# More warm-up products on TensorE, and five operations put elsewhere, at the start of a hybrid decoder layer

## The reference, cut to what matters

```python
xn = rmsnorm(h, norm_mix)
z = xn @ w_in                      # (1072 tokens x 1024) @ (1024 x 3592)
y_a = z[B] * causal_conv(z[C] * z[H])
q, k, v = silu(causal_conv(z[QKV]))
g    = -exp(a_log) * softplus(z[O_A:O_A + 4] + dt_bias)   # 4 columns of w_in
beta = sigmoid(z[O_A + 4:O_A + 8])                        # 4 more
o = gated_delta_rule(l2norm(q), l2norm(k), v, g, beta, state)
h = h + concat(y_a, rmsnorm(o) * silu(z[G])) @ w_out
h = h + relu(rmsnorm(h, norm_ffn) @ w_up) ** 2 @ w_down
y = rmsnorm(h, norm_final)
```

## Time and profile before

| | us |
|---|---|
| median of 3 runs | 1337.58 |
| lowest and highest | 1337.32, 1339.33 |
| the profiled execution's own time | 1337.32 |
| its span, first to last instruction | 1335.5 |
| PE busy in that span | 1315.9 (99%) |
| mean granted clock of PE | 0.998 |

### The profile page before, as it was taken

The page is one execution under the profiler, slowest core; times in us unless marked ns, Lnnn a source line. Parts: engine busy times, 40 slices in busy tenths (PEclk is TensorE's granted clock), DMA queues, the critical chain, the costliest instruction groups (busy, mean ns, idle before and its releaser), DMA issues.

```text
span 1335.5 us, 22540 instructions
## 1 busy us (share of the span) xinstructions
PE 1315.9 (99%) x9035; PEld 1287.1 (96%) x9035; DVE 832.0 (62%) x1406; ACT 410.8 (31%) x805; POOL 523.9 (39%) x544
## 2 busy tenths in 40 slices
PE   7999999999999999999999999999999999999997
PEld 6899999899999999999999999999999999999997
DVE  5566798435453665556666656756667567666855
ACT  6566552111221213231122222322223222223312
POOL 2322112111111111221367465574574756746811
PEclk9999999999999999999999999999999999999999
DMA  6223562743323323221101212112121121111202
GB/s 193 58 77 90 155 174 65 206 117 87 88 64 82 101 57 89 81 65 48 49 32 49 64 33 64 33 54 58 33 64 48 48 64 33 48 48 48 75 38 114
DMA packets 161850, 99.88 MB, mean 75 GB/s; under 512 B 19639, under 2 KB 156371, under 8 KB 161746
## 3 DMA queue, kind: packets, MB, share of 16 engines
q1 hardware_dynamic: 138770, 85.56, 21.8%
q10 hardware_dynamic: 22976, 12.88, 3.6%
HBM read 77.62 MB, written 20.80 MB: 74 GB/s over the span
## 4 chain that ended last, share of the span: by engine, by line
PE 96%; DVE 2%; ACT 1%; issue 0%; DMA 0%; ACTq 0%; POOL 0%; DVEq 0%
PE banks L1343 10%; PE banks L1345 10%; PE banks L1344 10%; PE banks L1854 9%; PE banks L1856 9%; PE banks L1855 9%; PE banks L1873 7%; PE banks L1874 7%; PE banks L1872 7%; PE banks L1888 1%; PE banks L1889 1%; PE banks L1890 1%; PE banks L1550 1%; PE banks L1564 1%; PE banks L1784 1%; PE banks L1466 1%
## 5 line engine op out<-in xcount | busy, mean ns | idle before, releaser
L1854 PE MATMUL banks<-hg_high,w_high 128*128 128x384 f32 (+1 forms) x768 | 249.5, 325 | 0.0
L1856 PE MATMUL banks<-hg_high,w_low 128*128 128x384 f32 (+1 forms) x768 | 247.6, 322 | 0.0
L1855 PE MATMUL banks<-hg_low,w_high 128*128 128x384 f32 (+1 forms) x768 | 247.3, 322 | 0.0
L2550 DVE TENSOR_TENSOR hT<-hT,banks 128x528 f32<-128x528 f32 x280 | 189.4, 701 | 84.4 <-PE banks L1874 77.3
L1343 PE MATMUL banks<-xn_high,w_high 128*128 128x384 f32 (+1 forms) x672 | 226.8, 337 | 0.8 <-DVE xn_low L1955 0.7
L1345 PE MATMUL banks<-xn_high,w_low 128*128 128x384 f32 (+1 forms) x672 | 218.1, 325 | 0.0
L1344 PE MATMUL banks<-xn_low,w_high 128*128 128x384 f32 (+1 forms) x672 | 217.9, 324 | 0.0
L786 POOL TENSOR_TENSOR w_low<-w_raw,w_high 128x1024 fp32r<-128x1024 f32 x31 | 77.0, 2483 | 244.4 <-ACT w_high L980 244.4
L1854 PEld LDWEIGHTS banks<-hg_high,w_high 128*128 128x128 f32 x768 | 144.2, 188 | 1.9 <-POOL w_low L912 1.7
L1855 PEld LDWEIGHTS banks<-hg_low,w_high 128*128 128x128 f32 x768 | 144.3, 188 | 0.1
L1856 PEld LDWEIGHTS banks<-hg_high,w_low 128*128 128x128 f32 x768 | 144.2, 188 | 0.0
(11 more groups left out here) (321 smaller groups left out, 2780.5 us busy)
## 6 DMA issues: line engine op xcount, KB each, us to landing
w_raw<-in_w_up SPq DMA_DIRECT2D x32, 512.0 KB, 4.0
w_pair<-in_w_down SPq DMA_DIRECT2D x32, 512.0 KB, 3.4
w_raw<-in_w_in SPq DMA_DIRECT2D x28, 512.0 KB, 4.3
w_raw<-in_w_out SPq DMA_DIRECT2D x8, 512.0 KB, 3.9
x_slice<-in_x_prompt SPq DMA_DIRECT2D x8, 512.0 KB, 4.1
out<-y_tok SPq DMA_DIRECT2D x8, 512.0 KB, 2.6
x_tok<-in_x_prompt SPq DMA_DIRECT2D x2, 1536.0 KB, 10.0
v_kept_rows<-v_feat SPq DMA_DIRECT2D x4, 536.0 KB, 2.9
```

The costliest lines, as they stand in the source:

```text
L1854: pe.matmul(bank[:, 0:w], w_h[half][:, k, :], hg_h[:, k, c0:c0 + w], start=(k == 0), stop=False)
L1855: pe.matmul(bank[:, 0:w], w_h[half][:, k, :], hg_l[:, k, c0:c0 + w], start=False, stop=False)
L1856: ins = pe.matmul(bank[:, 0:w], w_l[half][:, k, :], hg_h[:, k, c0:c0 + w], start=False, stop=(k == KT - 1))
L2550: dve.tensor_tensor(hc, hc, both, ALU.add if sign > 0 else ALU.subtract).then_inc(acc_read_dve, 1)
```

## The change

Six edits:

1. `IDLE_PRODUCTS` goes from (3, 1, 1) to (6, 4, 2): 7 more products ahead of tiles 0, 1 and 2.
2. SP issues `ab_raw` behind the two large loads of the tiles 3 to 8, not ahead of them.
3. ACT makes the high part of `ab` behind the square of tile 4, not right behind `split_high(0)`.
4. POOL makes the low part of `ab` behind the powers of tiles 0 to 5, not behind tile 2's.
5. DVE makes the low part of the first weight block behind the first `xn_low`, not ahead of it.
6. SP's send of the `v` rows goes from `g == 1` to `g == 2`, behind the load of a weight block.

PE's program is otherwise unchanged: `made_ab(0)` stays ahead of `turn_x(8)`.

```diff
-        IDLE_PRODUCTS = (3, 1, 1)
+        IDLE_PRODUCTS = (6, 4, 2)
...
-                if g == 1 and n >= 9 and IN_TILES[n - 1][0] == "v":
+                if g == 2 and n >= 9 and IN_TILES[n - 1][0] == "v":
...
                 if n == 0:
-                    sp.dma_start(ab_raw[:, :, :], w_in_v[:, :, O_A:O_A + 8]).then_inc(s_ahead, 16)
                     sp.dma_start(x_big[:, 2:5, :], xp_v[:, 2:5, :]).then_inc(s_xin[3], 16)
                     sp.dma_start(x_big[:, 5:8, :], xp_v[:, 5:8, :]).then_inc(s_xin[4], 16)
+                    sp.dma_start(ab_raw[:, :, :], w_in_v[:, :, O_A:O_A + 8]).then_inc(s_ahead, 16)
...
-            for t in range(NT):
+            for t in GTILES[0] + GTILES[1]:
                 x_power(t)
-                if t == 2:
-                    pool.wait_ge(ab_hi, 1)
-                    pool.tensor_tensor(ab_w[:, :, 8:16], ab_raw[:, :, :], ab_w[:, :, 0:8].bitcast(F32),
-                                       ALU.subtract).then_inc(ab_lo, 1)
+            pool.wait_ge(ab_hi, 1)
+            pool.tensor_tensor(ab_w[:, :, 8:16], ab_raw[:, :, :], ab_w[:, :, 0:8].bitcast(F32),
+                               ALU.subtract).then_inc(ab_lo, 1)
+            for t in GTILES[2]:
+                x_power(t)
...
             split_high(0)
-            act.wait_ge(s_ahead, 16)
-            act.activation(ab_w[:, :, 0:8], ab_raw[:, :, :], ACT.Copy).then_inc(ab_hi, 1)
...
                 for t in SQUARE_AFTER.get(m, ()):
                     square_x(t)
+                    if t == 4:
+                        act.wait_ge(s_ahead, 16)
+                        act.activation(ab_w[:, :, 0:8], ab_raw[:, :, :], ACT.Copy).then_inc(ab_hi, 1)
...
-            dve.wait_ge(w_high, 1)
-            dve.tensor_tensor(w_l[0][:, :, :], w_raw[0][:, :, :], w_h[0][:, :, :].bitcast(F32),
-                              ALU.subtract).then_inc(w_low, 1)
...
+                if m == 0:
+                    dve.wait_ge(w_high, 1)
+                    dve.tensor_tensor(w_l[0][:, :, :], w_raw[0][:, :, :], w_h[0][:, :, :].bitcast(F32),
+                                      ALU.subtract).then_inc(w_low, 1)
```

## The result

| | before | after |
|---|---|---|
| median of 6 runs each, us | 1337.51 | 1349.37 |
| lowest and highest | 1337.15, 1339.85 | 1347.35, 1352.31 |
| ratio, 95% interval | | 1.0078 [1.0061, 1.0093] |
| the profiled execution's own time | 1337.32 | 1350.52 |
| its span | 1335.5 | 1348.7 |

The change costs 11.9 us by the medians and 13.2 us between the two profiled executions. The ratio is taken over all executions on record, 23 of the kernel after (1345.33 to 1353.36 us, median 1347.69), and makes it 10.4 us. Each of these is at least twice the 5.0 us of my sum, and the time is outside my range.

The account below looks back on a forecast made before the run. TensorE was taken as the bound, its dense matmuls from 28.3 us on, so a late start is late at the end. 2.3 + 2.7 = 5.0 us on 1337.32, with the median's 0.26: 1342.5 us, range 1340.1 to 1344.1.

Parts of the forecast that it names:

- my sum: Whole kernel: 2.3 us for the later start of tile 2 plus 2.7 for the `ab` step, 5.0 us slower.
- my range: Whole kernel's time: the forecast's own range, 1340.1 to 1344.1 us around 1342.5.
- Edit 6: SP's v send behind a weight block's load: no PE stall to shorten from 70 to 200 us, 0, up to 0.3 either way.
- the clock falls in the new stall: Rival, chance 0.15: PE's clock drops while waiting ahead of `made_ab(0)`, at least +2.3 us, so 1344.9.
- d: Delay of tile 2's first transpose from seven more products ahead of it: +2.3 us (0.8 to 3.1, far end 5.5).
- The `ab` step: Late split of `ab` holds `made_ab(0)` and the transposes behind it: ninth high part +2.7 us (1.7 to 3.4) beyond d.
- POOL's low part: POOL's low part of `ab`, behind tile 5's power: taken near its old row of 1.21 us, ending at 22.2 plus d.
- Edit 5: DVE's weight split behind the first low part: 1.2 us by itself, partly hidden as an input of the `ab` step.
- Edit 2: `ab_raw` loaded behind the big loads: covered by eight high parts and two squares, cost 0, 0 to +1 us.
- the same busy time by stretch from 70 us on: Expected sign in the new profile: busy times by stretch unchanged from 70 us on.

Follow-up runs that it names:

- experiment 6: The whole changed kernel with only the fourth v send put back ahead of the weight load: 1345.66 us against 1338.99 before, ratio 1.0043.
- experiment 2: The kernel before with the late load and split of `ab` alone (edits 2, 3 and 4): 1340.78 us against 1337.81, ratio 1.0022.
- experiment 1: The kernel before with edit 6 alone, the v sends moved to `g == 2`: 1345.67 us against 1337.81, ratio 1.0056.
- second kernel of experiment 10: The kernel before with `turn_ab` in three parts and no idle products, (0, 0, 0): 1338.35 us against 1337.78, ratio 1.0002.
- experiments 5 to 8: Edit 6 plus products in its stall; change with fourth send back; `ab` step with transposes first; before with fewer products: 1342.37, 1345.66, 1340.88, 1337.42 us (first run).

## Why the prediction was wrong, by its steps

- **Edit 6, "PE has no stall from 70 to 200 us that an earlier load could shorten: 0, and as far as it goes, up to 0.3 either way": the step that failed.** Alone it costs 0.56% (7.5 us by the ratio). I asked what the load gains from going first, not who waits for the send that goes second. DVE's wait for the fourth send is one line of code, and SP's waits for the solve that now stand ahead of it are in the same step. I also looked at a window that ended at 200 us, while the send is used at 234. With the fourth send alone put back, the ratio of 1.0043 makes about 1343.3 us, inside my range; but that is partly luck, since the start was later there than I had summed.
- **The rival "the clock falls in the new stall": right as an extra, not in place of the sum.** The fall came behind the stall ahead of `made_ab(0)`, as said, at a price of 3.9 - 2.2 = 1.7 us against my 2.3. I had not asked it of any other place, since I had foreseen one stall. The clock falls also behind the second one, where in the profile of after it costs more than the wait (4.16 against 2.88 us), and behind `turn_ab` (+1.54), which may be chance.
- **d, +2.3 (0.8 to 3.1, far end 5.5): mis-sized for the profiled execution, and not a fixed number.** 0.9 after, 0.4 to 0.6 alone at the bound, 3.5 in experiment 6, all with the same products. The reason for the low end was the one given: the rise comes earlier. The sensitivity to it was right.
- **The `ab` step, +2.7 (1.7 to 3.4): inside its range by luck, from two errors of opposite sign.** The ninth high part is 4.27 us late (26.37 against 22.10). Without d of 0.9 that is 3.4, my high end; without the clock's 1.7 as well, 1.7 us are left, my low end. POOL's low part was the term too large: 1.21 assumed, 0.31 to 0.48 measured. It also started earlier than I had worked out, at 21.53 in after, which is 20.6 without d, against 21.05 to 21.7. With DVE's weight split no longer beside it, the low part is short. The Trainium skill ("SBUF — State Buffer", the part on the shared port pair) says that of a GpSimd operation that reads SBUF and a DVE operation with two SBUF inputs or in a two-port mode, the one that starts second is blocked until the other has ended. The numbers agree with it: 1.21 us beside a DVE operation with two SBUF inputs, ending 0.18 us behind it; 0.31 in experiment 2, where it started 0.07 us ahead of DVE's scaling.
- **Edit 5, hidden in the `ab` step: right.** PE waits 1.6 us for `w_low` where it waited 0.38, and alone it moves the bound by 0.2.
- **Edit 2, 0 to +1: right, with little room.** In experiment 2 `ab_raw` landed 12.6 us after its issue and ACT took it at once; in after it landed at 18.1 us (13.7 after its issue at 4.41), and ACT came for it at 19.11.
- **My own signs of error.** I had named "PE's stall ahead of `made_ab(0)` under 2 us" (it is 2.4), "tile 2 before 13" (13.36), and an end not late by as much as the two (it is later). None of these could catch edit 6. The sign that did was the last of the list before them, "the same busy time by stretch from 70 us on": it held to 200 us and broke at 245.

## What to carry to other kernels

When a DMA is moved, find every wait on its semaphore, and read the queue between its old and its new place for waits on other engines; a late wait in the same step is worse than the load it made way for. In this kernel every new stall of PE of 2.4 to 4.0 us came with a stretch at the lower clock, which at the stalls for `v_meta` cost as much again as the wait or more. So each stall in a forecast needs that term, with work for PE as the cure if the wait can't go. Work that fills a wait has a value that its own rows don't show: ask what the engine will do in that time once the work is elsewhere.

## What the runs showed of the hardware

- The lower level came back with PE never idle: 63.47 to 66.88 us after a row of 18 products of 16x8 in 2.13 us. The stretches at the lower level lasted 3.4 us in most places, 6.7 in experiment 2, and 10.2 behind the stalls for `v_meta` in after and experiment 1. In after PE was busy for 2.85 us of the first 3.42 of these and all the time from there on.
- In the second kernel of experiment 10 the clock rose at about 12.9 us, and all that PE had done until then were one small product (0.26 us) and 24 transposes, the last sixteen of them in a row of 3.68 us. The Trainium skill ("TensorE: Matmul & The Clock Gate", Part 4) says that transposes don't count as activity; this trace does not agree.
- PEclk reads 1.00 ahead of the first rise, although the rows there show the lower level: 16 transposes in 3.68 us, 0.23 each, against 0.11 at the upper one.
- Executions of one kernel differ by 2 to 5 us (before: 1337.15 to 1339.85 at first, 1336.97 to 1342.10 beside experiments 5 to 8). A fall of 3.4 us at the lower level costs 1.5 to 1.7 us, and profiles of kernels that share the instructions at that place have one or not. That these falls make the spread fits, but isn't shown.
